# Experts get 96 row slots each: twelve steps of four 32-row blocks instead of sixteen steps of 128 rows, and a loop for rows past 96

## The chip, the cores and the metric

The kernel runs on one core of a Trainium2 chip. The metric is the device time of one execution in microseconds (us). The engines are named as in the profile: PE is TensorE (PEld its weight loads, that is the loads of its stationary operand), DVE VectorE, ACT ScalarE, POOL GpSimd, SP SyncE; a q behind a name is the engine's own queue of DMA issues and register work. All data is f32.

## The reference, cut to what matters

576 tokens (512 of a prompt, 64 of a sample) go through one layer: two recurrent branches and an output projection, then a mixture of experts, then a per-layer input embedding. The part around the change:

```python
grp = jnp.argmax(grp_logits, axis=-1)                      # top-1 group of 4
in_grp = ...                                               # the 4 experts of that group
top_v, top_i = lax.top_k(in_grp, TOP_K)                    # top 2 of them
w_top = jax.nn.softmax(top_v, axis=-1) * p_grp
...
for e in range(N_EXPERTS):                                 # 16 experts
    gu = jnp.einsum('bld,df->blf', u, w_gate_up[e])        # 1024 -> 512
    hid = jax.nn.silu(gu[..., :D_EXPERT]) * gu[..., D_EXPERT:]
    moe = moe + combine[..., e:e + 1] * jnp.einsum('blf,fd->bld', hid, w_down[e])   # 256 -> 1024
h = h + moe
u = rmsnorm(h, norm_ple)
h = h + jax.nn.sigmoid(u @ w_ple_gate) * (p_l @ w_ple_proj)
```

Each token uses two experts, so 1152 rows are spread over 16 experts. On the reference's inputs they fall as 65, 98, 80, 95, 44, 47, 51, 58, 61, 79, 68, 72, 88, 68, 87 and 91 rows.

## The kernel before, in words

Up to about 595 us the kernel does the branches, the output projection ("wo"), and the router. The router works tile by tile (five tiles of tokens, order 4, 1, 0, 3, 2): it ranks each token within its expert ("rank"), and turns ranks into a list of tokens for each expert with small matmuls ("ids"). The steps are written out by hand in `schedule()`; every engine walks that one list and does its part of each step. Two further kinds of step, "ovp" on DVE and "idv" on PE, prepare lists for rows past 128.

The expert stage works on 16 experts, one after the other, 128 row slots each. For expert e:

- POOL gathers its 128 token rows from `u_rows` in DRAM into `xg` (L2567; empty slots get row 0 with weight 0).
- PE transposes them into PSUM (`xpose`, L1222), DVE scales them into `xT` (L2284).
- PE does gate/up: 8 matmuls, k by k, with the 128 slots as stationary operand and 512 columns of `w_gu` moving, into PSUM bank `single[3]` (L1250). An f32 matmul leaves two records in the trace.
- ACT does SiLU (L1618), DVE the product (L2277, `hid`), PE two transposes (L1263), ACT copies them to `hT`.
- PE does down, 4 matmuls of 512 columns (L1234, `down`), but one expert later; ACT copies the result to `yb` and SP stores it to `y_slots` in DRAM.

Weights live in four buffers, one for an expert: gate/up 2 MB and down 1 MB. SP loads expert e+4 into the buffer of expert e right behind the store of e's result (`after_expert`, L667 to L670), which waits for that result. The first two experts are loaded during the router and before it, the third and fourth once the first two gathers have landed (L660).

After the last expert PE makes the p products of four tiles (L1290), reads from the table `ovi` how many blocks of rows past 128 there are, and goes through a loop over them (L1304 and following; SP, POOL, ACT and DVE have their halves of it; SP fetches the weights, POOL the rows). Then comes the tail: for each tile (order 0, 1, 4, 2, 3) POOL gathers the two rows of each token from `y_slots` (L2598), DVE adds them up (L2322, semaphore `h3`), PE transposes (L1336) and multiplies with `w_pg` (L1352), and ACT and DVE finish the tile. Gathers of the third and later tiles wait for the sum two tiles before.

## Time and profile before

| | |
|---|---|
| median of 3 runs | 873.87 us (873.84 to 874.2) |
| profiled execution, first to last instruction | 872.5 us |
| PE busy | 854.9 us, 98% |
| DVE / ACT / POOL busy | 388.7 / 223.3 / 155.1 us |
| DMA moved | 135.98 MB, mean 156 GB/s |
| granted PE clock, mean | 0.997 |

The profiled execution has no separate time of its own beside its span; the 1.4 us between the span and the median of the runs lie before the first and after the last instruction. Busy PE means that matmuls are under way; it is a share over stages with different limits, so the stages have to be read one by one.

### The profile page before, as it was taken

Reading aid. Unit: us, or ns where it says so; the run is one execution under the profiler, and the core shown is the slowest. Engines: PE = TensorE matmul, PEld = TensorE weight load, DVE = VectorE, ACT = ScalarE, POOL = GpSimd, SP = SyncE. Lnnn points to the kernel's source line nnn. Section 1 sums busy time; section 2 is a strip of 40 time slices with the busy share of each in tenths; the row PEclk is TensorE's granted clock in tenths of the full one; section 3 lists DMA queues with packets and bytes.
Section 4 is the critical chain, followed back from the end, with each engine's and each line's share of the span. In section 5 each row is a group of like instructions: output and inputs, shape, how many; then the busy total and the mean of one; then the engine's idle time right before and its main releaser. Section 6 shows DMA issues by size and latency. Waiting matters only on the chain.

```text
span 872.5 us, 11853 instructions
## 1 busy us (share of the span) xinstructions
PE 854.9 (98%) x4645; PEld 556.1 (64%) x4645; DVE 388.7 (45%) x857; ACT 223.3 (26%) x478; POOL 155.1 (18%) x186
## 2 busy tenths in 40 slices
PE   8999999999999999999999999999999999999996
PEld 4546777888799877777777764565444444444452
DVE  3223566677546324566734577364211111104553
ACT  2202152265224210121011101230311111125454
POOL 0324420022243314201300250002000000003000
PEclk9999999999999999999999999999999999999998
DMA  9521343502020201334132221157999999685211
GB/s 362 188 85 65 134 124 134 151 1 105 1 99 3 98 1 44 163 111 150 55 139 96 97 97 76 49 193 276 393 373 371 367 365 371 251 319 169 71 38 48
DMA packets 19814, 135.98 MB, mean 156 GB/s; under 512 B 2512, under 2 KB 3024, under 8 KB 12592
## 3 DMA queue, kind: packets, MB, share of 16 engines
q1 hardware_dynamic: 12176, 103.28, 30.9%
q0 software_dynamic: 5424, 26.45, 8.7%
q10 hardware_dynamic: 2160, 5.51, 2.1%
q8 instruction: 37, 0.61, 0.3%
q14 instruction: 17, 0.14, 0.1%
HBM read 117.83 MB, written 21.60 MB: 160 GB/s over the span
## 4 chain that ended last, share of the span: by engine, by line
PE 43%; DVE 3%; issue 2%; ACT 1%; DMA 1%; POOLq 0%; POOL 0%; DVEq 0%; ACTq 0%
PE single L1250 13%; PE pair L1234 6%; PE pair L1151 6%; PE single L914 6%; PE pair L1352 3%; PE pair L935 2%; PE single L1222 2%; PE pair L1290 2%; PE single L935 2%; PE single L1199 1%; DMA mem<-y_slots,posu 1%; PE single L1160 1%; DVE mem L2322 0%; PE single L1263 0%; DVE mem L2082 0%
## 5 line engine op out<-in xcount | busy, mean ns | idle before, releaser
L734 PE MATMUL pair<-mem 128*128 128x288 f32 x640 | 158.9, 408 | 0.0
L734 PEld LDWEIGHTS pair<-mem 128*128 128x128 f32 x640 | 120.3, 190 | 35.6 <-ACT mem L1373 2.1
L1250 PE MATMUL single<-mem 128*128 128x512 f32 x256 | 112.8, 593 | 0.8 <-DVE mem L2284 0.8
L914 PE MATMUL single<-mem 128*128 128x288 f32 x448 | 110.0, 407 | 0.3
L914 PEld LDWEIGHTS single<-mem 128*128 128x128 f32 x448 | 84.7, 190 | 25.7 <-issue 1.6
L1250 PEld LDWEIGHTS single<-mem 128*128 128x128 f32 x256 | 47.3, 190 | 54.1 <-issue 53.1
L1373 ACT ACTIVATE mem<-single 128x256 f32<-128x256 f32 (+5 forms) x113 | 46.5, 421 | 133.2 <-PE single L1160 48.7
L1373 ACT ACTIVATE mem<-pair 128x512 f32<-128x512 f32 (+5 forms) x85 | 37.8, 495 | 164.0 <-PE pair L734 63.1
L2277 DVE SCALAR_TENSOR_TENSOR mem<-single,mem 128x256 f32<-128x256 f32 x16 | 7.7, 483 | 138.8 <-PE single L1250 126.3
L1352 PE MATMUL pair<-mem 128*128 128x512 f32 (+1 forms) x192 | 63.4, 524 | 1.1 <-DVE mem L2332 1.1
L1234 PE MATMUL pair<-mem 128*128 128x512 f32 x128 | 57.7, 593 | 0.5 <-ACT mem L1373 0.5
L1151 PE MATMUL pair<-mem 128*128 128x512 f32 x112 | 51.0, 601 | 0.0
L1352 PEld LDWEIGHTS pair<-mem 128*128 128x128 f32 (+1 forms) x192 | 28.3, 172 | 33.3 <-issue 28.8
L2007 DVE TENSOR_TENSOR mem<-mem,single 128x288 f32<-128x288 f32 x40 | 18.1, 452 | 55.7 <-PE single L914 52.2
L2567 POOL DMA_INDIRECT mem<-u_rows,ids x16 | 15.8, 990 | 144.1 <-PE single L1222 134.0
L1234 PEld LDWEIGHTS pair<-mem 128*128 128x128 f32 x128 | 23.1, 190 | 24.1 <-issue 23.4
L1151 PEld LDWEIGHTS pair<-mem 128*128 128x128 f32 x112 | 20.3, 190 | 21.7 <-issue 21.4
L1618 ACT ACTIVATE mem<-single,mem 128x256 f32<-128x256 f32 x16 | 7.6, 475 | 103.6 <-PE single L1250 103.6
L809 PE MATMUL pair<-mem 128*128 128x512 f32 (+1 forms) x96 | 32.1, 525 | 0.0
L785 PE MATMUL pair<-mem 128*128 128x512 f32 x64 | 28.2, 595 | 0.9 <-DVE mem L1722 0.9
L935 PE MATMUL pair<-mem 128*128 128x288 f32 x112 | 28.4, 409 | 0.2
L1808 DVE SCALAR_TENSOR_TENSOR mem<-mem,vec 128x512 f32<-128x512 f32 x36 | 27.9, 774 | 1.3
(394 smaller groups left out, 1152.3 us busy)
## 6 DMA issues: line engine op xcount, KB each, us to landing
mem<-in_w_gu SPq DMA_DIRECT2D x16, 2048.0 KB, 9.1
mem<-in_w_down SPq DMA_DIRECT2D x16, 1024.0 KB, 11.8
y_slots<-mem SPq DMA_DIRECT2D x16, 512.0 KB, 3.7
y_slots<-in_zeros POOLq DMA_DIRECT2D x8, 512.0 KB, 8.4
mem<-in_w_ga SPq DMA_DIRECT2D x2, 2048.0 KB, 8.6
mem<-in_w_gb SPq DMA_DIRECT2D x2, 2048.0 KB, 8.4
mem<-in_w_wo SPq DMA_DIRECT2D x2, 2048.0 KB, 8.1
mem<-in_w_pg SPq DMA_DIRECT2D x2, 2048.0 KB, 11.5
```

Source lines behind the costliest of these rows:

```text
L734: last = nc.tensor.matmul(pb[:, hf, 0:HALF], w(k), rhs[:, k, hf * HALF:(hf + 1) * HALF], start=(k == 0), stop=(k == kk - 1))
L785: last = nc.tensor.matmul(q_bank[t][rows, cols], uT[:, k, t * P:t * P + ntok(t)], ring[0][:, 512 * k + cols.start:512 * k + cols.stop], st ...
L809: last = nc.tensor.matmul(pair[plan.buf[s]][rows, 0, cols], uT[:, k, t * P:t * P + ntok(t)], w[:, k, cols], start=(k == 0), stop=(k == KD ...
L914: last = nc.tensor.matmul(single[plan.buf[s]][:, 0:HALF], lhs[:, k, :], rhs[:, k, :], start=(k == 0 and j in (0, 1, 3, 4)), stop=(k == 3), ...
L935: last = nc.tensor.matmul(fast_bank(s), lhs[:, k, :], rhs[:, k, :], start=(k == 0 and j in (0, 1, 3, 4)), stop=(k == 1), skip_group_check= ...
L1151: last = nc.tensor.matmul(sx_bank[j], rows[:, u, v, :], wgt[:, u, 512 * v:512 * v + 512], start=(i == 0 and j < 5), stop=(i == 3), skip_gr ...
L1234: last = nc.tensor.matmul(pair[u % 2][:, n, :], hT[u % 2][:, k, :], w_dn[u][:, k, n * 512:(n + 1) * 512], start=(k == 0), stop=(k == 1))
L1250: last = nc.tensor.matmul(single[3][:, :], xT[u % 2][:, k, :], w_gu[u][:, k, :], start=(k == 0), stop=(k == KD - 1))
L1352: last = nc.tensor.matmul(pair[(k + 1) % 2][rows, hf, cols], u3T[:, c, t * P:t * P + n], w_pg[hf][:, c, cols], start=(c == 0), stop=(c == ...
L1373: copy = lambda out, in_, scale=1.0: nc.scalar.activation(out, in_, ACT.Copy, scale=scale)
L1808: V.scalar_tensor_tensor(out=acc[m % 2][:, 0:LP], in0=cbuf[m % 2][:, j:j + LP], scalar=conv_w[:, m, j:j + 1], in1=acc[m % 2][:, 0:LP], op0 ...
L2007: V.tensor_tensor(to, plus, single[plan.buf[s]][:, 0:HALF], ALU.add).then_inc(ev(k0), 1)
```

## The change

Each expert gets 96 slots (`CAP`) in blocks of 32 (`BS`). 16 x 96 = 1536 slots make 12 steps (`NPH`) of 128 slots. A step p has four blocks, each with its own expert: step 0 has three of expert 0 and one of expert 1, step 1 two of expert 1 and two of expert 2, step 2 one of expert 2 and three of expert 3, and so on in cycles of three steps and four experts. Gathers, transposes, DVE, ACT and stores work as before on 128 slots, twelve times. The matmuls of gate/up and down are cut into four, one for each 32 slots, each with the weights of its own expert moving and its own 32 rows of PSUM.

```diff
+def blocks_of(p):
+    return [((4 * p + g) // 3, (4 * p + g) % 3, g) for g in range(4)]
+def last_phase(e):
+    return (3 * e + 2) // 4
@@ PE, gate/up and down
-                    last = nc.tensor.matmul(single[3][:, :], xT[u % 2][:, k, :], w_gu[u][:, k, :],
-                                            start=(k == 0), stop=(k == KD - 1))
+                    for e, _, g in blocks_of(p):
+                        last = nc.tensor.matmul(single[3][BS * g:BS * g + BS, :], xT[p % 2][:, k, BS * g:BS * g + BS],
+                                                w_gu[e % 4][:, k, :], start=(k == 0), stop=(k == KD - 1))
...
-                        last = nc.tensor.matmul(pair[u % 2][:, n, :], hT[u % 2][:, k, :], w_dn[u][:, k, n * 512:(n + 1) * 512],
-                                                start=(k == 0), stop=(k == 1))
+                        for e, _, g in blocks_of(p):
+                            last = nc.tensor.matmul(pair[p % 2][BS * g:BS * g + BS, n, :], hT[p % 2][:, k, BS * g:BS * g + BS],
+                                                    w_dn[e % 4][:, k, n * 512:(n + 1) * 512], start=(k == 0), stop=(k == 1))
```

SP no longer waits for an expert's result before it reloads its gate/up weights, only for the step that used them last:

```diff
-            def after_expert(e, u, more):
-                sp.wait_ge(sem("y_ready"), 2 * e + 2)
-                sp.dma_start(y_slots[bass.ds(e * P, P), :], yb[u % 2]).then_inc(sem(f"y_stored{u % 2}"), 16)
-                if more:
-                    sp.dma_start(w_gu_flat[u], ...)
-                    sp.dma_start(w_dn_flat[u], ...)
+            for p in range(NPH - 1):
+                sp.wait_ge(sem("gu_mm"), p + 1)
+                for e in range(NEXP - 4):
+                    if last_phase(e) == p:
+                        load_gu(e + 4)
+                if p == NPH - 2:
+                    sp.dma_start(view(BLK, CHUNK_W), a["w_pg0"]).then_inc(sem("w_pg"), 16)
+                if p:
+                    store(p - 1)
+                for e in range(NEXP - 4):
+                    if last_phase(e) == p - 1:
+                        load_dn(e + 4)
+                if p == NPH - 3:
+                    sp.dma_start(w_proj.rearrange("p k c -> p (k c)"), a["w_proj"]).then_inc(sem("w_proj"), 16)
```

The preparation for rows past the slots moves out of the router: "ovp" and "idv" leave `schedule()`, and in their place DVE computes the lists behind step 0 and PE multiplies them out (ten matmuls of 64 columns) in step 1. The lists of slots for gathers are laid out by copies of 32 to 96 partitions:

```diff
-                    V.tensor_copy(ids[:, 0:NEXP], idp[0][:, 0:NEXP]).then_inc(sem("ids"), 1)
-                    V.tensor_copy(rsl[:, 0:NEXP], idp[0][:, NEXP:2 * NEXP]).then_inc(sem("ids"), 1)
+                    runs = {0: [(0, 0, 0, 96), (1, 0, 96, 32)], 1: [(1, 32, 0, 32), (1, 64, 32, 32), (2, 0, 64, 64)],
+                            2: [(2, 64, 0, 32), (3, 0, 32, 32), (3, 32, 64, 32), (3, 64, 96, 32)]}
+                    for v, dst in enumerate((ids, rsl)):
...
+                                last = V.tensor_copy(to[at:at + n, :, q], src[lo:lo + n, :, e])
+                            if v == 0:
+                                last.then_inc(sem("ids"), 1)
```

The loop for the rest takes blocks of 32 rows past 96 (up to 32 blocks, before 8 of 128 rows past 128) and now stands ahead of the p products. SP loads the block's expert anew; the weights move in four parts of the output columns, one to each column group, with the same 32 rows stationary:

```diff
+                    sp.dma_start(w_gu_flat[0], a["w_gu"][bass.ds(e * P, P), :]).then_inc(sem("ov_w"), 16)
+                    sp.dma_start(w_dn_flat[0], a["w_down"][bass.ds(e * P, P), :]).then_inc(sem("ov_w"), 16)
@@ PE, ahead of the p products
+                    pe.wait_ge(sem("ov_dve"), 2 * i + 1)
+                    pe.wait_ge(sem("ov_w"), 32 * i + 32)
+                    for k in range(KD):
+                        for g in range(4):
+                            last = nc.tensor.matmul(single[3][BS * g:BS * g + BS, 0:P], xT_ov[:, k, :], w_gu[0][:, k, P * g:P * g + P],
+                                                    start=(k == 0), stop=(k == KD - 1))
...
+                            last = nc.tensor.matmul(single[1][BS * g:BS * g + BS, 0:DE], hT_ov[:, BS * k:BS * k + BS],
+                                                    w_dn[0][:, k, DE * g:DE * g + DE], start=(k == 0), stop=(k == 1))
@@ ACT, the block's result
+                    for g in range(4):
+                        act.dma_start(y_slots[bass.ds(i * BS + NEXP * CAP, BS), DE * g:DE * g + DE], y_ov[BS * g:BS * g + BS, :])\
+                            .then_inc(sem("ov_stored"), 16)
@@ POOL, ahead of the tail's gathers
+                    pool.wait_ge(sem("ov_stored"), 64 * i + 64)
+                    pool.sem_inc(sem("ov_free"), 1)
```

How PE's program moves, at a place in the middle of the expert stage. Before, one expert (gate/up, transposes of the next expert's rows, down of the expert before, hidden transposes):

```order
L1250 MATMUL single<-mem 128x512 [waits hid,wgu1,xT]
L1250 MATMUL single<-mem 128x512 x7
L1222 MATMUL single<-const,mem 128x128 [waits xT,xg0]
L1222 MATMUL single<-const,mem 128x128 x7
L1234 MATMUL pair<-mem 128x512 [waits y_ready,hT]
L1234 MATMUL pair<-mem 128x512 x3
L1263 MATMUL single<-const,mem 128x128 [waits hid]
L1263 MATMUL single<-const,mem 128x128
```

Now one step, here one that uses the weight buffers 2 and 3:

```order
L1275 MATMUL single<-mem 32x512 [waits wgu3,hid,wgu2,xT]
L1275 MATMUL single<-mem 32x512 x31
L1245 MATMUL single<-const,mem 128x128 [waits xT,xg0]
L1245 MATMUL single<-const,mem 128x128 x7
L1260 MATMUL pair<-mem 32x512 [waits wdn2,y_ready,wdn1,hT]
L1260 MATMUL pair<-mem 32x512 x15
L1286 MATMUL single<-const,mem 128x128 [waits hid]
L1286 MATMUL single<-const,mem 128x128
```

The order is the same; gate/up and down have four times the instructions, and each step waits for the weights of two experts, gate/up and down apart.

SP's queue from the first reload on, now (three steps, then on in the same way):

```order
L680 DMA mem<-in_w_gu 128x4096 [waits gu_mm]
L680 DMA mem<-in_w_gu 128x4096
L702 DMA y_slots<-mem 128x1024 [waits y_ready]
L683 DMA mem<-in_w_down 128x2048
L680 DMA mem<-in_w_gu 128x4096 [waits gu_mm]
L702 DMA y_slots<-mem 128x1024 [waits y_ready]
L683 DMA mem<-in_w_down 128x2048 x2
L680 DMA mem<-in_w_gu 128x4096 [waits gu_mm]
L702 DMA y_slots<-mem 128x1024 [waits y_ready]
L683 DMA mem<-in_w_down 128x2048
```

Before, every expert had the same three rows there; two of them:

```order
L667 DMA y_slots<-mem 128x1024 [waits y_ready]
L669 DMA mem<-in_w_gu 128x4096
L670 DMA mem<-in_w_down 128x2048
L667 DMA y_slots<-mem 128x1024 [waits y_ready]
L669 DMA mem<-in_w_gu 128x4096
L670 DMA mem<-in_w_down 128x2048
```

Gate/up loads moved ahead of the store, down loads stay behind it, and four experts' loads now go with three stores.

PE's program behind the last down, before:

```order
L1290 MATMUL pair<-mem 128x512 [waits y_ready,w_proj,ld_p]
...
L1299 TENSOR_LOAD ovi [waits y_ready,ov_ready]
...
L1308 MATMUL single<-const,mem 128x128 [waits ov_xg]
...
L1313 MATMUL single<-mem 128x512 [waits ov_w]
...
L1336 MATMUL single<-const,mem 128x128 [waits h3]
```

and now:

```order
L1291 TENSOR_LOAD ovi [waits ov_ready]
...
L1297 MATMUL single<-const,mem 128x32 [waits ov_xg]
...
L1303 MATMUL single<-mem 32x128 [waits ov_w]
L1303 MATMUL single<-mem 32x128 x31
...
L1308 MATMUL single<-const,mem 128x64 [waits ov_dve]
...
L1312 MATMUL single<-mem 32x256 [waits ov_act]
L1312 MATMUL single<-mem 32x256 x7
...
L1330 MATMUL pair<-mem 128x512 [waits y_ready,w_proj,ld_p]
...
L1344 MATMUL single<-const,mem 128x128 [waits h3]
```

The loop (L1297 to L1312) moved from behind the p products (L1290, now L1330) to ahead of them.

## Rows read from the trace of the kernel before

**Rows 1.** Windows by stage: busy us of each engine, clock, DMA share, GB/s.

```profile
560.00:597.00 37.00, 35.73 (x186) 20.66 (x184) 21.77 (x88) 6.97 (x18) 4.32 (x5) 1.00 0.41 143
597.00:780.84 183.84, 183.37 (x549) 89.82 (x550) 33.07 (x82) 31.29 (x66) 13.89 (x16) 1.00 0.91 354
780.84:795.00 14.16, 13.74 (x33) 5.73 (x32) 2.57 (x2) 4.55 (x6) 4.04 (x5) 1.00 0.65 227
795.00:872.50 77.50, 69.25 (x248) 33.48 (x248) 38.15 (x60) 42.48 (x71) 6.29 (x6) 0.97 0.20 66
```

**Rows 2.** Chain that ended last, around two experts: start us, us, what.

```profile
606.59 6.87 PE single L1250 x16
...
652.18 6.87 PE single L1250 x16
659.05 0.87 PE single L1222 x8
659.92 3.44 PE pair L1234 x8
663.36 0.22 PE single L1263 x2
```

**Rows 3.** Windows, as in rows 1: weights alone, and ten steady experts.

```profile
608.00:612.00 4.00, 4.00 (x10) 1.71 (x9) 2.67 (x15) 0.00 (x0) 0.00 (x0) 1.00 1.03 418
641.70:755.70 114.00, 114.00 (x341) 55.59 (x340) 16.78 (x30) 18.41 (x41) 8.43 (x9) 1.00 0.95 367
```

**Rows 4.** Timeline of PE: start us, us to its last end, group.

```profile
96.70 2.19 PE L795 MATMUL pair<-mem 128*32 128x288 f32 x32
98.81 3.42 PE L734 MATMUL pair<-mem 128*128 128x288 f32 x13
...
580.20 0.65 PE L1169 MATMUL single<-mem,w_rt 128*32 128x128 f32 x16
```

**Rows 5.** Timelines of PE and DVE near the last router tiles.

```profile
581.36 0.71 PE L744 MATMUL pair<-mem 64*128 64x128 f32 x4
...
582.51 0.24 DVE L2153 SCALAR_TENSOR_TENSOR lg<-single,ms,vec 128x20 f32<-128x20 f32 x1 [0.74 <-PE single L1175]
```

**Rows 6.** Timeline of SP's DMA queue, the third expert's weights.

```profile
597.51 0.33 SPq L660 DMA_DIRECT2D mem<-in_w_gu  x1
```

**Rows 7.** DMA issues from 597 to 781 us: count, KB each, us to landing.

```profile
y_slots<-mem SPq DMA_DIRECT2D x15, 512.0 KB, 3.6
```

**Rows 8.** Timelines of DVE and PE, and ACT's groups by shape.

```profile
590.38 0.17 DVE L2204 TENSOR_SCALAR placeu<-placeu 128x6 uint32<-128x6 uint32 x1
590.87 0.96 DVE L2207 TENSOR_TENSOR mem<-mem,kr 128x768 f32<-128x768 f32 x1
...
308.69 1.08 PE L1089 MATMUL single<-mem 128*32 128x128 f32 x32
...
L1618 ACT ACTIVATE mem<-single,mem 128x256 f32<-128x256 f32 x16 | 7.6, 475 | 103.6 <-PE single L1250 103.6
L1373 ACT ACTIVATE mem<-single 128x128 f32<-128x128 f32 x2 | 0.5, 272 | 0.6 <-PE single L1169 0.6
```

**Rows 9.** Chain that ended last, end of the expert stage.

```profile
780.84 13.73 PE pair L1290 x32
...
795.00 1.11 PE single L1336 x8
```

**Rows 10.** Timeline of POOL, two gathers of the tail.

```profile
786.58 0.98 POOL L2598 DMA_INDIRECT mem<-y_slots,posu  x1 [22.47 <-SPq L701]
...
794.79 0.91 POOL L2598 DMA_INDIRECT mem<-y_slots,posu  x1 [3.46 <-DVE mem L2322]
```

**Rows 11.** The page's instruction queues (packets, MB, share), and a window of dense matmuls.

```profile
q8 instruction: 37, 0.61, 0.3%
q14 instruction: 17, 0.14, 0.1%
...
200.00:300.00 100.00, 98.39 (x1420) 88.33 (x1419) 56.71 (x141) 35.20 (x84) 34.41 (x51) 1.00 0.19 66
```

More of the change, by code:

```diff
@@ L736, in gemm_channels @@
                 last.then_inc(s_mm, 1)
-            def overflow_ids(t):
-                i, n = POS[t], ntok(t)
-                pe.wait_ge(sem("pickm"), 1 if i < 2 else 2)
-                for j in range(2):
-                    at = 128 * (2 * i + j)
-                    last = nc.tensor.matmul(idp[1], pickm[0:n, i, j, :], eov[0:n, at:at + 128],
-                                            start=(i + j == 0), stop=(i + j == NT))
-                return last
             pe.wait_ge(sem("rtmp_ones"), 1)
@@ L1208, in _, with overflow_ids @@
                     ev_wait(pe, s)
-            def late_overflow_ids():
-                for t in ORDER[2:]:
-                    last = overflow_ids(t)
-                last.then_inc(sem("idv_mm"), 1)
-            def xpose(n_gather, n_prev, u):
-                pe.wait_ge(sem(f"xg{u % 2}"), n_gather)
-                if n_prev is not None:
-                    pe.wait_ge(sem("xT"), n_prev)
+            def overflow_ids():
+                pe.wait_ge(sem("eov"), 1)
+                for c in range(2 * NT):
+                    n = ntok(ORDER[c // 2])
+                    last = nc.tensor.matmul(idp[1], pickm[0:n, c, :],
+                                            eov[0:n, c].rearrange("p v b -> p (v b)"), start=(c == 0), stop=(c == 2 * NT - 1))
+                last.then_inc(sem("ovi_mm"), 1)
@@ L1220, in xpose, with down @@
+            def xpose(p):
+                pe.wait_ge(sem(f"xg{p % 2}"), 16 * (p // 2 + 1))
+                if p:
+                    pe.wait_ge(sem("xT"), p)
                 for k in range(KD):
                     out = single[k // 4][:, (k % 4) * P:(k % 4 + 1) * P]
-                    last = nc.tensor.transpose(out, xg[u % 2][:, k * P:(k + 1) * P], C("ident"))
+                    last = nc.tensor.transpose(out, xg[p % 2][:, k * P:(k + 1) * P], C("ident"))
                 last.then_inc(sem("xT_mm"), 1)
-            def down(e, u, first):
-                pe.wait_ge(sem("hT"), e + 1)
-                if not first:
-                    pe.wait_ge(sem("y_ready"), 2 * e - 2)
-                elif u == 1:
-                    pe.wait_ge(sem("ids"), 4)
+            def down(p):
+                pe.wait_ge(sem("hT"), p + 1)
+                for e in experts_of(p):
+                    pe.wait_ge(sem(f"wdn{e % 4}"), 16 * (e // 4 + 1))
+                if p >= 2:
+                    pe.wait_ge(sem("y_ready"), 2 * p - 2)
+                if p == 1:
+                    pe.wait_ge(sem("ov_ready"), 3)
@@ new lines, in _ @@
+            xpose(0)
+            for p in range(NPH):
+                pe.wait_ge(sem("xT" if p else "xT_half"), p + 1)
+                for e in experts_of(p):
+                    pe.wait_ge(sem(f"wgu{e % 4}"), 16 * (e // 4 + 1))
+                if p:
+                    pe.wait_ge(sem("hid"), p)
+                for k in range(KD):
+                    if p == 0 and k == 4:
+                        xpose(1)
+                    for e, _, g in blocks_of(p):
+                        last = nc.tensor.matmul(single[3][BS * g:BS * g + BS, :], xT[p % 2][:, k, BS * g:BS * g + BS],
+                                                w_gu[e % 4][:, k, :], start=(k == 0), stop=(k == KD - 1))
+                last.then_inc(sem("gu_mm"), 1)
+                if 0 < p < NPH - 1:
+                    xpose(p + 1)
+                if p == 1:
+                    overflow_ids()
+                if p:
+                    down(p - 1)
+                pe.wait_ge(sem("hid"), p + 1)
@@ L1262, in expert @@
                 for k in range(2):
-                    last = nc.tensor.transpose(single[2][:, k * P:(k + 1) * P], hid[u % 2][:, k * P:(k + 1) * P], C("ident"))
+                    last = nc.tensor.transpose(single[2][:, k * P:(k + 1) * P], hid[p % 2][:, k * P:(k + 1) * P], C("ident"))
                 last.then_inc(sem("hT_mm"), 1)
-            xpose(16, None, 0)
-            for e in range(4):
-                expert(e, e, True, True, (16 * ((e + 1) // 2 + 1), 32))
-            with pe.Fori(1, 3) as i:
-                for u in range(4):
-                    expert(4 * i + u, u, True, False, ((i * 2 + (u + 1) // 2 + 1) * 16, i * 32 + 32))
```

415 lines of the change are left out of this document (190 added, 225 removed).

## The prediction

> **What bounds the kernel now.** I read the windows by stage first [rows 1]. In the expert stage, 597.0 to 780.8 us, TensorE is busy 183.37 of 183.84 us at the full granted clock (1.00, the 2.4 GHz level); the DMA engines are busy 0.91 of it. Then come 14.2 us of p products (a matmul stage of four tiles) and 77.5 us of tail with DMA nearly idle. The chain that ended last [rows 2] runs through TensorE alone there and shows one expert: 6.87 us of gate/up, 0.87 of transposes, 3.44 of down, 0.22 of hidden transposes, 11.40 us in all, sixteen times. So TensorE sets the stage. But DMA is close behind: in ten steady experts its share is 0.95 at 367 GB/s, and where it has a backlog of weights it is 1.03 (full) at 418 GB/s [rows 3]. A change that shortens TensorE's part by a quarter therefore meets the DMA engines, and the sum has to be made for both.
>
> **Does the new shape run at the old speed?** A step has 4 x 8 gate/up matmuls with 32 stationary columns and 512 moving ones where an expert had 8 with 128. If the four column groups run at once, gate/up still takes 6.87 us; one after another, 27.5. The trace of before has 32-column matmuls: L795, 32 records of 288 moving columns with four different moving operands, begins at 96.70 and the next group begins at 98.81 [rows 4]. (A matmul in f32 leaves two records.) L734 behind it, 128 columns wide with the same 288 moving, starts a record every (3.42 - 0.41) / 12 = 0.25 us, 0.41 being the mean of one. 32 x 0.25 = 8.0 us in turn, 2.0 at four at a time; it took 2.11. So the groups overlap, and 0.1 to 0.2 us goes at the change of shape. L1169 says the same: 16 records of 128 columns are over in 0.65 us; in turn they would take 16 x 128 / 288 x 0.25 = 1.8. A step changes shape four times; I charge 0.1 each, 0.4. Step = 11.40 + 0.4 = 11.8 us.
>
> The Trainium skill has a measured figure that speaks against this ("TensorE: Matmul & The Clock Gate", Part 3, Packing small matmuls): four 32-row tiles with 512 moving columns gave 3.07x, not 4x, and column tiling behaves within some ns of that. By it a step would be about 10.3 / 0.77 + 1.5 = 14.9 us. L795's 8.0 / 2.11 = 3.8x, its shape change included, disagrees, so the sum keeps 11.8.
>
> **TensorE's side.** Before the stage the change drops two matmul groups (idv) and two pieces of DVE work (ovp), and cuts the id copy into small ones. Only the idv of tile 4 shows on the path: DVE stood 0.74 us for the transposes (L1175) queued right behind it [rows 5]. The copy for gather 0 is now two copies; call it +0.1. I take 0.5 us off: step 0's gate/up starts at 596.5. Step 0 has gate/up and a transpose but no down: G0 (its end of gate/up) = 604.9, and step 1 starts at 606.4 after SiLU, hidden product and transposes, as before (606.59) [rows 2]. Step 1 carries the ten small matmuls that place rows past 96, +1.0. The DVE work for them is about 18 small operations at 0.17 to 0.2 us and 2,560 elements of wide ones at the rate of L2207 (768 in 0.96) [rows 8]: 6.5 us, from 606.1 to 612.6, before TensorE asks at 614.5: hidden behind step 1's gate/up, margin 2 us; without that cover it would delay down(0) one for one. If weights were always there, gate/up of step p would end at G1 = 613.4, then every 11.8 (step 1 being a us longer): G5 = 661.7, G11 = 732.5, last down at about 741.
>
> **The DMA side.** Sixteen experts' weights are still 3.146 MB each; only gathers and stores fall from 16 to 12. The third expert's load is issued at 597.51 after the first gathers have landed [rows 6], unchanged by the diff. From there to the end of the weights that the row loop at the end needs, the engines must move: 14 experts 44.0 MB, w_proj 1.05, w_pg0 2.1, pT 0.6, one expert again for the loop 3.15: 50.9 MB at 418 GB/s = 121.8 us. A store plus a gather costs what the steady experts leave [rows 3]: 11.4 x 0.95 - 3.146 / 0.418 = 3.3 us a pair; ten pairs = 33 us. Sum 154.8: 597.5 + 154.8 = 752.3, plus 1.5 to 2 us to land (a lone store lands in 3.6 us though it is 1.8 of work) [rows 7]: **754.5**. This holds only if the queue is never empty. I followed it: loads of expert e+4 go out when e's last gate/up is over, its down weights some 6 us later behind the store. At each issue 6 us or more of older work is still queued (gu5 goes out at 613.4, the queue is full to 621; gu6 and gu7 at 626.4, full to 634; later 10 us), so it isn't.
>
> Put together, TensorE waits twice: step 6 for expert 9, which lands at 670 instead of the wanted 666.5, and step 9 for expert 13, at 710.5 instead of 705. That gives G9 = 717.5, G10 = 729.3, G11 = 741, last down over at **749**, where before has 780.84 [rows 9]. The stage alone is 32 us shorter; TensorE without waits would be 40.
>
> **The loop at the end.** Routing the reference's own inputs gives 98 rows for expert 1 and at most 95 for any other: one block of 32 is past 96, none was past 128, and before's loop shows no instruction. The body runs once. SP issues its weights near 735.5, behind dn15, w_proj, w_pg0 and store 9, hence 754.5. TensorE does its 8 transposes before and then waits 5 to 6 us. Then: 64 records of 128 columns at four at a time 1.8 to 2.1 us (L1089, half as many, 1.08 to its last end), SiLU and copy 0.45, product 0.25, transpose 0.3, copy 0.25, 16 records of 256 columns 0.95, five hops 0.3, register work 0.2: 4.5 us, so it ends at 759. Before ran the p products (13.73 us) straight after the last down; now they run 759 to 772.8. Beside them: copy 0.4, four DMA issues on ACT 1.4 (at SP's 0.33), landing about 3 on busy engines, POOL's pT4 0.75, so tile 0's first gather starts near 765 instead of 786.58. From it to the next gather that waits for tile 0's sum is 8.2 us in before (794.79 [rows 10]): 773.5. That is 0.7 us later than the products, and the tail (L1336) starts at **774** instead of 795.0. w_pg1 and the norm land near 765. The tail is untouched: 77.5 us. Span 872.5 - 21 = 851.5; the runs' median stands 1.4 us over the profiled span, so 852.9; I round up to **853.5** for hops not counted.
>
> **Rivals.** (1) Column groups overlap worse, as the skill's figure says. By rows: gate/up and down take 1.3 times their 10.3 us, a step is 14.9; DMA no longer limits; last down 613.4 + 1 + 10 x 14.9 + 9 = 772, tail starts 18.9 later at 791, time 870. For it: no row has four groups of 512 columns under a full DMA load. Against: L795. 0.08, and 0.12 for halfway, 13 us a step: last down 753 by the same sum, but the block's weights come at 754.5 anyway, time 855 to 862. (2) Slower: TensorE starves for instructions. The stage has some 2,700 instructions for it, all unrolled. At 16 KB a packet and some 64 bytes an instruction (0.75 MB on the two instruction queues [rows 11] for the page's 11,853) that is 11 fetches, behind full DMA engines; with smaller packets up to 20. If each of 15 stopped it for a store's landing, 3.6 us, that is 54 us: last down 741 + 54 = 795, tail at 814, time 893. It decides from 2.3 us a fetch, 35 us in all. Against: between 200 and 300 us TensorE took 1420 matmul records, 14 a us, and was busy 98.39, where this stage asks 9 a us; but DMA was 0.19 then. 0.06; all slower cases 0.08. (3) The DMA reckoning is off: a share of 0.95 instead of full adds 8 us: 861; 0.12, in the range. (4) The loop doesn't run, because the counts differ: the products start at 749, the gathers 5.7 us later as in before, tail near 763.5: 843; 0.05. A second block would instead cost a serial 17 us (weights 7.5, landing 2, body 4.5, store 3), 870; 0.02. (5) Forecast, 849 to 857: 0.55.
>
> **How the numbers follow.** The likeliest case gives 853.5. The low end takes in part of the case without a block and a full rate a little above 418, 845; the high end takes in the DMA at 0.95 and the halfway case with some tail cost, 864. The rest lies above. Within 0.2% (1.7 us, about what a measurement tells) only rival 1 with extras: 0.03. Faster 0.89, slower 0.08.
>
> **What would show it.** After: 32x512 groups with 64 records in 6.9 to 7.1 us; waits for weights at steps 6 and 9 of 3 to 5 us and none before; DMA share over 0.97 from 600 to 755; the loop's gate/up released by a DMA near 755; p products about 14 us after 759; tail start near 774 and 77.5 long. It is wrong if a step is longer than 13 us without a weight wait, if gaps on TensorE are put down to issue, if DMA falls idle in the stage, or if the last gathers come later than the products.

## The result and the profile after

| | before | after |
|---|---|---|
| time, median of 4 runs, us | 874.04 (873.84 to 875.23) | 848.81 (846.25 to 851.14) |
| profiled execution: time, span, us | (above) | 849.0, 847.2 |
| ratio after / before | | 0.9705 [0.9682, 0.9728] |
| mean granted clock | | 0.994 |

The kernel became 2.95% faster, 4.7 us more than forecast. The windows of the changed kernel, from the first expert step to the tail (span, then busy us of PE, PEld, DVE, ACT and POOL, granted clock, DMA share, GB/s), answer to [rows 1, 3]:

```profile
597.00:641.70 44.70, 43.43 (x382) 16.24 (x386) 17.38 (x56) 7.90 (x15) 3.73 (x5) 1.00 1.00 405
641.70:744.30 102.60, 101.86 (x906) 33.34 (x898) 13.56 (x24) 16.09 (x35) 7.37 (x10) 1.00 1.01 418
744.30:749.00 4.70, 0.69 (x12) 0.57 (x8) 0.42 (x1) 1.08 (x2) 0.00 (x0) 0.95 1.04 437
749.00:752.50 3.50, 3.35 (x64) 2.88 (x64) 0.00 (x0) 0.00 (x0) 0.00 (x0) 0.57 0.99 420
...
755.30:758.00 2.70, 2.70 (x8) 1.15 (x5) 0.00 (x0) 0.39 (x1) 0.00 (x0) 0.52 0.27 94
...
761.00:771.00 10.00, 10.00 (x26) 4.45 (x25) 2.57 (x2) 2.77 (x3) 5.04 (x6) 1.00 0.62 216
```

Read them down. From 641.7 to 744.3 two resources are full at once: TensorE is busy 101.86 of 102.60 us, the DMA share is 1.01. Then TensorE stands still for 4.1 us, and the clock is at 0.57 and 0.52, near its lower level (0.50, 1.2 GHz), in the windows in which it next has much work; after 761 it is back at 1.00. The chain that ended last shows one step, and what replaced the old end of the stage [rows 2, 9]:

```profile
644.99 0.37 PE single L1286 x2
645.35 7.00 PE single L1275 x64
652.36 1.02 PE single L1245 x8
653.38 3.57 PE pair L1260 x32
...
733.15 15.89 DMA mem<-in_w_down
749.08 3.40 PE single L1303 x64
...
755.34 15.63 PE pair L1330 x32
770.96 0.87 PE single L1344 x8
```

A step takes 7.00 + 1.02 + 3.57 + 0.37 = 11.96 us, 11.97 from one start to the next, against 11.40 for an expert before. The block's weights, landing at 749.05, release the loop; the p products run to 770.96, and behind them come 847.2 - 770.96 = 76.2 us of tail, where before had 77.5. The chain stays on TensorE there until 839.9 us; the last 7.3 us are ACT's and DVE's work on the last tile. The table of waits says how little TensorE waited between 600 and 772 us (us in total, times, longest):

```profile
PE single L1303 <- DMA mem<-in_w_down: 4.1, 1, 4.1
...
PE single L1275 <- DMA mem<-in_w_gu: 0.3, 1, 0.3
```

One wait for an expert's weights in twelve steps, of 0.3 us (step 9, at 705.46). What full engines do to the transfers stands in the DMA summary of 590 to 760 us (count, KB each, us from issue to landing):

```profile
y_slots<-mem SPq DMA_DIRECT2D x12, 512.0 KB, 11.1
...
mem<-u_rows,ids POOLq DMA_INDIRECT x12, 11.0
y_slots<-mem ACTq DMA_DIRECT2D x4, 32.0 KB, 1.5
```

A store of 512 KB that landed in 3.6 us before [rows 7] now takes 11.1, and a gather 11.0. The engines move 405 to 418 GB/s meanwhile, so this isn't slower work but a longer line. Nothing on TensorE waits for them in the stage, because each is asked for a whole step ahead.

### The profile page after: what moved, and what is told of

Its sections match the earlier page's. It is cut to its first block and busy times, and to the rows that moved or that the text cites. A ratio compares the mean times of both kernels' runs of the same rounds, so it can differ in the third digit from the quotient of the medians.

```text
span 847.2 us, 13448 instructions
## 1 busy us (share of the span) xinstructions
PE 822.9 (97%) x5462; PEld 519.9 (61%) x5462; DVE 385.5 (46%) x857; ACT 215.2 (25%) x464; POOL 152.6 (18%) x184
## 5 line engine op out<-in xcount | busy, mean ns | idle before, releaser
L765 PEld LDWEIGHTS pair<-mem 128*128 128x128 f32 x640 | 120.3, 190 | 35.6 <-ACT mem L1381 2.1
L935 PE MATMUL single<-mem 128*128 128x288 f32 x448 | 110.0, 407 | 0.3
L935 PEld LDWEIGHTS single<-mem 128*128 128x128 f32 x448 | 84.7, 190 | 25.7 <-issue 1.6
L1275 PE MATMUL single<-mem 128*32 128x512 f32 x768 | 85.1, 594 | 1.1 <-DVE mem L2304 0.9
L1381 ACT ACTIVATE mem<-pair 128x512 f32<-128x512 f32 (+5 forms) x77 | 33.5, 485 | 156.7 <-PE pair L765 63.0
L1275 PEld LDWEIGHTS single<-mem 128*32 128x32 f32 x768 | 24.0, 110 | 52.7 <-issue 51.6
L2297 DVE SCALAR_TENSOR_TENSOR mem<-single,mem 128x256 f32<-128x256 f32 x12 | 5.8, 484 | 104.3 <-PE single L1275 91.4
L1172 PE MATMUL pair<-mem 128*128 128x512 f32 x112 | 51.0, 601 | 0.0
L1260 PE MATMUL pair<-mem 128*32 128x512 f32 x384 | 43.7, 595 | 0.5 <-ACT mem L1381 0.5
L1172 PEld LDWEIGHTS pair<-mem 128*128 128x128 f32 x112 | 20.3, 190 | 21.7 <-issue 21.4
L2586 POOL DMA_INDIRECT mem<-u_rows,ids x12 | 11.4, 947 | 110.5 <-PE single L1245 100.5
L806 PE MATMUL pair<-mem 128*128 128x512 f32 x64 | 28.2, 595 | 0.8 <-DVE mem L1735 0.8
L956 PE MATMUL single<-mem 128*128 128x288 f32 x112 | 27.8, 406 | 0.0
## 6 DMA issues: line engine op xcount, KB each, us to landing
mem<-in_w_down SPq DMA_DIRECT2D x17, 1024.0 KB, 14.9
y_slots<-mem SPq DMA_DIRECT2D x12, 512.0 KB, 11.1
```

Source lines behind the costliest of these rows:

```text
L765: last = nc.tensor.matmul(pb[:, hf, 0:HALF], w(k), rhs[:, k, hf * HALF:(hf + 1) * HALF], start=(k == 0), stop=(k == kk - 1))
L806: last = nc.tensor.matmul(q_bank[t][rows, cols], uT[:, k, t * P:t * P + ntok(t)], ring[0][:, 512 * k + cols.start:512 * k + cols.stop], st ...
L935: last = nc.tensor.matmul(single[plan.buf[s]][:, 0:HALF], lhs[:, k, :], rhs[:, k, :], start=(k == 0 and j in (0, 1, 3, 4)), stop=(k == 3), ...
L956: last = nc.tensor.matmul(fast_bank(s), lhs[:, k, :], rhs[:, k, :], start=(k == 0 and j in (0, 1, 3, 4)), stop=(k == 1), skip_group_check= ...
L1172: last = nc.tensor.matmul(sx_bank[j], rows[:, u, v, :], wgt[:, u, 512 * v:512 * v + 512], start=(i == 0 and j < 5), stop=(i == 3), skip_gr ...
L1260: last = nc.tensor.matmul(pair[p % 2][BS * g:BS * g + BS, n, :], hT[p % 2][:, k, BS * g:BS * g + BS], w_dn[e % 4][:, k, n * 512:(n + 1) * ...
```

## The experiments

My theory after the result: (T1) the gain is TensorE's alone, twelve steps of 12.0 us instead of sixteen of 11.4; (T2) DMA doesn't set the stage though its share is 1.01, it sets only what stands behind it, the block's weights; (T3) the 4.1 us wait and the slow clock behind it are the loop's real price. Rivals: the column groups lose time by themselves; the gain comes from the new order of SP's loads; DMA sets the stage. Ratios are to the kernel before, with runs on the same chip; intervals are 95%.

**a_cols: before, with column groups and nothing else.** Sixteen experts of 128 slots, each matmul of gate/up and down cut into four groups of 32.

```diff
-                    last = nc.tensor.matmul(single[3][:, :], xT[u % 2][:, k, :], w_gu[u][:, k, :],
-                                            start=(k == 0), stop=(k == KD - 1))
+                    for g in range(0, P, 32):
+                        last = nc.tensor.matmul(single[3][g:g + 32, :], xT[u % 2][:, k, g:g + 32], w_gu[u][:, k, :],
+                                                start=(k == 0), stop=(k == KD - 1))
... (down in the same way)
```

> The kernel before, sixteen experts of 128 slots, with one part of the change alone: gate/up and down are cut into four matmuls of 32 stationary columns each (same weights four times). Theory 1 (column groups overlap fully, a change of shape costs 0.14 us as in the changed kernel's trace): an expert takes 11.40 + 0.56 = 11.96 us, the stage grows by 16 x 0.56 = 9 us, time near 883. Rival (the overlap is poorer when the moving operand is read by four groups under full DMA, and the changed kernel hides it in fewer steps): by the skill's 3.07 of 4, 3.1 us an expert, time near 923. Second rival (instructions run short): gaps on TensorE put down to issue, some us each.

Measured: 885.14 us (882.46 to 885.9), 1.0106 [1.0084, 1.0129]. Its chain, and a window of ten experts:

```profile
752.75 7.00 PE single L1252 x64
759.75 1.02 PE single L1222 x8
760.78 3.57 PE pair L1235 x32
764.35 0.37 PE single L1265 x2
```

```profile
641.70:761.00 119.30, 119.30 (x1060) 39.58 (x1056) 16.84 (x31) 18.35 (x40) 9.05 (x10) 1.00 0.91 351
```

The reader is to see the same four durations as in the changed kernel, and gate/up and down with four times as many matmul records as in [rows 2], at 11.96 us an expert instead of 11.40. Each of the four groups is 0.13 to 0.15 us longer than in before, and that is all; TensorE is never idle in the window, so no instruction comes late. I had put 883. The cutting by itself costs 1.1%; it pays only because a quarter of the steps goes.

**g_before_order: before, with the new order of loads and nothing else.** SP asks for gate/up weights when the last gate/up that used the buffer is over, ahead of the store.

```diff
-            for e in range(4):
-                after_expert(e, e, True)
...
+            for e in range(13):
+                if e < 12:
+                    sp.wait_ge(sem("gu_mm"), e + 1)
+                    sp.dma_start(w_gu_flat[e % 4], a["w_gu"][(e + 4) * P:(e + 5) * P, :]).then_inc(sem(f"wgu{e % 4}"), 16)
+                if e:
+                    after_expert(e - 1, (e - 1) % 4, False)
+                    sp.dma_start(w_dn_flat[(e - 1) % 4], a["w_down"][(e + 3) * P:(e + 4) * P, :]).then_inc(sem(f"wgu{(e - 1) % 4}"), 16)
```

> The kernel before with the other part of the change alone: gate/up weights of expert e+4 are issued when e's gate/up is over, down weights behind the store of the next step, all loads and stores of SP unrolled. Theory 1 (TensorE sets the stage before, loads come in time anyway): same time, 874, DMA share 0.95 as before. Rival (the gain of the changed kernel comes in part from a fuller DMA queue): some us faster.

Measured: 875.25 us (873.82 to 877.15), 1.0008 [0.9996, 1.0019]. No effect: TensorE had its weights in time without it.

**e_half: the changed kernel with half of each gate/up load left out** for experts 4 to 15 (the columns not loaded hold the weights of an earlier expert, so these experts compute with partly wrong weights). 12.6 MB less, TensorE's work unchanged.

```diff
-                sp.dma_start(w_gu_flat[e % 4], a["w_gu"][e * P:(e + 1) * P, :]).then_inc(sem(f"wgu{e % 4}"), 16)
+                c = CHUNK_W if e < 4 else CHUNK_W // 2
+                sp.dma_start(w_gu_flat[e % 4][:, 0:c], a["w_gu"][e * P:(e + 1) * P, 0:c]).then_inc(sem(f"wgu{e % 4}"), 16)
```

> The changed kernel with half of each gate/up load left out for experts 4 to 15 (the other half of the buffer keeps the weights of four experts earlier), so that 12.6 MB less move; the loop's own load is whole. TensorE's program is the same. Theory 1 (TensorE sets the stage at 12 us a step, DMA only the loop's wait): the last down ends at 744 as before, the loop's weights are there, clock stays full; time 842, the same as moving w_pg. Rival (the full DMA engines set the stage): 12.6 MB at 415 GB/s are 30 us, the stage ends near 715 to 720, time near 820.

Measured: 844.88 us (844.63 to 846.28), 0.9659 [0.9636, 0.9681]. One window of its stage, its last down (L1261) and the loop's gate/up, and the last down of the changed kernel (L1260):

```profile
600.00:740.00 140.00, 138.80 (x1231) 47.24 (x1223) 30.32 (x77) 22.58 (x47) 10.19 (x13) 1.00 0.87 332
...
740.90 3.64 PE L1261 MATMUL pair<-mem 128*32 128x512 f32 x32 [0.47 <-ACT mem L1382]
...
747.25 2.00 PE single L1304 x64
...
740.74 3.64 PE L1260 MATMUL pair<-mem 128*32 128x512 f32 x32 [0.47 <-ACT mem L1381]
```

With DMA at 0.87 instead of full, the last down ends where it did: 147.0 us behind the start of step 0 (597.58), in the changed kernel 147.3 (597.07), and the 0.3 us are its one wait. DMA doesn't set the stage (T2 holds; otherwise 12.6 MB less, some 30 us at 417 GB/s, would have shown). The 4 us come from behind it, 3 less than I had put (842): the block's weights land 1.8 us earlier, the wait is 2.1 us, and the loop's gate/up takes 2.00 us instead of 3.40, at full clock.

**b_noloop: the changed kernel with the number of blocks set to 0**; it leaves out the two rows of expert 1 past 96. **c_order: w_pg0 loaded behind the block's weights**, not ahead of them. **d_warm: five matmuls of 512 columns that nobody reads, in the wait.**

```diff
 b: count of blocks
-float(BS - 1 - CAP), 0.0, ALU.add, ALU.max
+-4096.0, 0.0, ALU.add, ALU.max
 c: SP
-                if p == NPH - 2:
-                    sp.dma_start(view(BLK, CHUNK_W), a["w_pg0"]).then_inc(sem("w_pg"), 16)
...
                     sp.dma_start(w_dn_flat[0], a["w_down"][bass.ds(e * P, P), :]).then_inc(sem("ov_w"), 16)
+            sp.dma_start(view(BLK, CHUNK_W), a["w_pg0"]).then_inc(sem("w_pg"), 16)
             store(NPH - 2)
 d: PE, in the loop
+                    for _ in range(5):
+                        nc.tensor.matmul(single[2][:, :], C("ones"), h2[:, 0, 0:512], start=True, stop=True)
                     pe.wait_ge(sem("ov_dve"), 2 * i + 1)
                     pe.wait_ge(sem("ov_w"), 32 * i + 32)
```

> The changed kernel with the count of blocks past 96 forced to zero, so that the loop is skipped; it leaves out the two rows of expert 1 past its 96 slots. It prices the whole loop. Theory 1 (the loop costs its wait for weights 4.1, its body 6.3, and 1.9 of slower p products, but without it the tail's first gathers become late): last down at 744.3, products over at 758, first sum at 760, span 836, time 838, 11 us less. Rival (DMA sets the end of everything, and the loop's weights only stand in a queue that is full anyhow): the tail waits for w_pg and the stores, time no lower than 843.

> The changed kernel with one load moved: the first w_pg chunk is issued behind the loop's weights instead of ahead of them. Theory 1 (the loop waits 4.1 us because 5.0 us of w_pg stands ahead of its weights in the queue, and the idle time then lowers the clock): weights land at 744, no wait, clock 1.00 throughout, body 4.5 us, products 13.7 us, time near 842. Rival A (the clock falls for another reason, such as the loop's small matmuls): the wait is gone but the body and the products keep 3.4 and 15.6 us, time 844.5. Rival B (w_pg becomes late for the tail): time as the changed kernel's, 849.

> The changed kernel with five matmuls of 512 columns, results unused, put in the wait for the loop's weights (4.3 us of work in a wait of 4.1). It changes nothing but what TensorE does in the wait. Theory 1 (the idle wait lowers the granted clock, 0.57 in two stretches behind it, and that costs 1.6 us in the loop's gate/up and 1.9 in the p products): those come back, gate/up 1.9 us, products 13.7 us, time 3 us less, near 846. Rival (the body is slow through its instructions and hops, and the clock plays no part): no change, 849.

Measured: b 846.17 us (843.44 to 847.49), 0.9673 [0.9656, 0.9689]; c 848.36 us (847.99 to 850.77), 0.97 [0.9681, 0.972]; d 848.09 us (847.4 to 848.57), 0.9687 [0.9671, 0.9703]. All three intervals touch that of the changed kernel, 0.9705 [0.9682, 0.9728]: b may be a little faster, c and d can't be told from it. I had put b at 838, c at 842 and d at 846 (its rival at 849): b and c are misses, and for d the times don't tell the two cases apart. The traces say more, if one thing is kept in mind. The profiled executions reach the expert stage at different times, though the edits of c and d lie behind that point and b's changes one constant: step 0's first matmul starts between 597.07 and 600.44 us (the latest is j_noloop's, below). So times of two traces are compared here as they stand behind that start:

| | step 0 starts | tail starts | from one to the other | step 0 to the end of the span |
|---|---|---|---|---|
| before | 596.98 | 795.00 | 198.0 | 275.5 |
| changed kernel | 597.07 | 770.96 | 173.9 | 250.1 |
| b_noloop | 598.56 | 763.65 | 165.1 | 243.0 |
| c_order | 598.23 | 768.53 | 170.3 | 248.4 |
| d_warm | 599.14 | 770.24 | 171.1 | 247.6 |
| e_half | 597.58 | 766.23 | 168.7 | 245.3 |

These are single executions; two of the changed kernel (here and after_again below) differ by 0.4 to 0.5 us. First d, two windows of it:

```profile
749.00:752.00 3.00, 3.00 (x38) 1.52 (x40) 0.00 (x0) 0.00 (x0) 0.00 (x0) 1.00 1.04 440
...
755.00:758.00 3.00, 3.00 (x21) 1.38 (x22) 0.00 (x0) 0.38 (x1) 0.00 (x0) 1.00 0.51 200
```

The same program on a TensorE that was kept busy: clock 1.00 where it was 0.57 and 0.52. Its chain, with its start of step 0 first and TensorE's p products from its timeline last:

```profile
599.14 3.64 PE single L1275 x32
...
746.71 4.49 PE single L1300 x10
751.20 1.93 PE single L1305 x64
...
758.09 2.03 DMA y_slots<-mem
...
763.31 5.50 DMA mem<-y_slots,posu
...
770.24 1.09 PE single L1346 x8
...
755.91 14.00 PE L1332 MATMUL pair<-mem 128*128 128x512 f32 x32
```

The loop's gate/up is 1.93 us, not 3.40, and the products take 14.00, not 15.7: the idle wait was what lowered the clock, both times. Counted from step 0 the products end at 170.8 instead of 173.9, 3.1 us earlier, and the tail starts 2.8 us earlier: the clock's price is as T3 had it, though the run times show no more than a hint of it. The last 0.3 us are missing because it is no longer the p products that release the tail: it is the loop's result, stored, gathered and summed. Behind the loop stand **two chains**, PE's products and store, gather, sum. In the changed kernel the second ended with this sum:

```profile
767.87 1.28 DVE L2338 SCALAR_TENSOR_TENSOR mem<-mem,wcomb 128x1024 f32<-128x1024 f32 x1 [1.35 <-DMA mem<-y_slots,posu]
```

It is over at 769.15, 1.8 us before the products. Shortening the products alone gives only that distance; whatever the loop's body gains, both chains gain. c_order's chain says it louder:

```profile
746.39 1.99 PE single L1302 x64
...
753.35 5.39 DMA y_slots<-mem
...
767.19 1.30 DVE mem L2337
...
768.53 1.24 PE single L1343 x8
769.77 3.36 PE pair L1329 x16
...
770.00:771.00 1.00, 1.00 (x6) 0.47 (x4) 1.00 (x2) 0.00 (x0) 0.86 (x1) 0.50 0.58 131
```

Here the wait for weights is gone (gate/up starts at 746.39, 3.9 us earlier counted from step 0) and the clock is 1.00 in the loop. But w_pg0 and w_pg1 are still moving when the block's result, four pieces of 32 KB, wants to be stored: a piece lands 5.0 us after its issue (median, the last one 5.39), 1.5 in the changed kernel. The tail waits 3.4 us for the sum, and behind this wait the clock is at 0.50 again (from 770 to 772 us; the last line is the window of its first us): the 16 matmuls of L1329 take 3.36 us, 1.88 in the changed kernel. So the tail starts 3.6 us earlier and the end is only 1.8 us earlier. T3 is wrong in its size: wait and clock together, 7 us, are not to be had by moving this load. In b, without a loop, the last step's store takes the same place, queued behind w_pg1:

```profile
746.70 8.27 DMA y_slots<-mem
...
757.09 5.13 DMA mem<-y_slots,posu
...
763.65 1.97 PE single L1344 x8
```

The Trainium skill ("DMA: Bandwidth & Descriptors", Issuing engines are not separate DMA queues) says that transfers of SP, ACT and POOL run on the same 16 engines and interleave, whoever issued them. These rows agree: ACT's own queue did not keep 32 KB pieces clear of SP's 2 MB loads, 5.0 us beside them against 1.5 without.

**f_two: a second block, which finds no rows.** It tells what a block costs where nothing hides it.

```diff
-float(BS - 1 - CAP), 0.0, ALU.add, ALU.max
+float(BS + 1 - CAP), 0.0, ALU.add, ALU.max
```

> The changed kernel with the block count rounded up two rows earlier, so that expert 3 with 95 rows gets a block too (an empty one) and the loop runs twice. It prices one more block. Theory 1 (a further block is serial: store landed, weights issued, 7.5 us of load and 2 to land, body 6 us, then its own store): 17 to 20 us more, time 866 to 869. Rival (the second block overlaps with the p products or the stores): under 10 us more.

Measured: 872.8 us (871.29 to 874.48), 0.9972 [0.9959, 0.9985]: 24 us more than with one block, where I had put 17 to 20. Its chain from the first block's result on:

```profile
760.62 1.47 DMA y_slots<-mem
...
763.53 10.66 DMA mem<-in_w_down
774.23 3.57 PE single L1303 x64
...
780.66 15.63 PE pair L1330 x32
```

From one block's gate/up (751.02) to the next (774.23) are 23.2 us: body 8.0 to 759.0, issue and store 3.1, SP's turn 1.4, weights 10.7. SP asks for the second block's weights only when the first one's result is stored, so nothing overlaps, and the clock is low again (3.57, 15.63). Almost the whole gain of the change is gone with the second block.

**h_best: c_order with pT4 issued behind the first gathers on POOL. i_pool: c_order, and w_pg1 and pT4 issued by POOL behind the second tile's gathers**, so that they are in nobody's way before the tail; PE waits for w_pg1 where it first needs it. **j_noloop: b_noloop with the last store ahead of w_pg1** (leaves out the same two rows). **after_again: the changed kernel once more**, on the chip of i and j.

```diff
 i: SP
-            sp.wait_ge(sem("gu_mm"), NPH)
-            sp.dma_start(view(BLK + 12288, CHUNK_W), a["w_pg1"]).then_inc(sem("w_pg"), 16)
             store(NPH - 1)
 i: POOL, in the tail's gathers
+                if k == 1:
+                    pool.wait_ge(sem("dn_mm"), NPH)
+                    pool.wait_ge(sem("ld_p"), 16)
+                    pool.dma_start(pT4, a["pT"][:, :, 4 * P:TOK]).then_inc(sem("ld_p"), 16)
+                    pool.dma_start(view(BLK + 12288, CHUNK_W), a["w_pg1"]).then_inc(sem("ld_iota"), 16)
 j: SP
+            store(NPH - 1)
             sp.dma_start(view(BLK + 12288, CHUNK_W), a["w_pg1"]).then_inc(sem("w_pg"), 16)
-            store(NPH - 1)
```

> The changed kernel with w_pg behind the loop's weights and, besides, POOL's small load pT4 moved behind the first two gathers of the tail. Theory 1: 842 from the order, and 0.5 to 0.8 us less if the first sum of the tail is what its start waits for then: 841 to 842. Rival (the gathers have slack): as the order alone.

> The changed kernel with the loop's weights ahead of the first w_pg chunk, and with the second w_pg chunk and pT4 taken from their places ahead of the tail's gathers and issued by POOL behind the gathers of the second tile. Theory (the tail starts at the later of two chains: TensorE's p products, and the loop's result stored, gathered and summed; moving w_pg alone won nothing since its loads then lay on that store, 5.4 us to land instead of 2.0, and on the last step's store): the store lands in 2 to 3 us, first gathers at 757 instead of 761, products over and first sum both near 765, against 771.0 in the changed kernel; time 843. Rival (the gathers are held by something else, and the second chain stays at 769): time 847.

> The kernel without the loop (it leaves out the two rows past 96) with the last step's store issued ahead of the second w_pg chunk instead of behind it. Theory of the two chains: without the loop the tail waited for the last store, which took 8.3 us behind w_pg; now it lands in some 3 us, first gathers at 751, first sum near 758.5, products over at 759.5: tail starts at 759.5 instead of 763.6, time 842. Rival: as the kernel without the loop, 846.

> The changed kernel itself on the same chip, for the comparison with the two others: 848 to 849.

| | median us | ratio to before | span us | tail starts | behind the start of step 0 | step 0 to the end |
|---|---|---|---|---|---|---|
| h_best | 846.61 (845.98 to 847.42) | 0.9676 [0.9654, 0.9698] | 844.2 | 767.75 | 169.3 | 245.8 |
| i_pool | 846.15 (845.58 to 848.41) | 0.9675 [0.9661, 0.9689] | 844.9 | 765.28 | 167.0 | 246.6 |
| j_noloop | 842.12 (841.42 to 844.13) | 0.9623 [0.961, 0.9636] | 842.3 | 764.29 | 163.9 | 241.9 |
| after_again | 850.28 (848.89 to 851.65) | 0.9722 [0.9709, 0.9736] | 847.1 | 770.79 | 173.4 | 249.7 |

i_pool and h_best are the fastest versions that compute everything: i_pool is 0.5% below the changed kernel on the same chip (0.9675 / 0.9722 = 0.995, intervals apart). The two can't be told apart. Both missed what I had hoped from the chains (841 to 842, and 843); j_noloop came as forecast (842). In i_pool the forecast up to the tail came true:

```profile
751.35 13.93 PE pair L1327 x32
765.28 0.89 PE single L1341 x8
```

But its tail is 844.9 - 765.28 = 79.6 us, 3.4 longer than the changed kernel's 76.2, and its table of waits from 765 to 845 us shows where:

```profile
PE pair L1359 <- DVE mem L2347: 2.0, 2, 1.1
PE pair L1327 <- DMA mem<-in_pT: 1.1, 1, 1.1
```

The first row is TensorE waiting for DVE. DVE's sums waited 6.2 us for gathers in that stretch (2.7 in the changed kernel's tail), and a gather took 6.7 us to land (5.3), while w_pg1 took 12.2 on the same engines. That w_pg1 is what makes them late is likely, but no run takes it apart. In j the store is quick, and the gather behind it pays instead:

```profile
748.59 3.05 DMA y_slots<-mem
...
753.75 9.11 DMA mem<-y_slots,posu
```

Store 8.27 and gather 5.13 in b, store 3.05 and gather 9.11 in j: 13.4 and 12.2 us. Where the 2 MB are queued decides who waits for them, and hardly how long. j's own gain over b is 0.5%, with intervals that don't overlap (0.9623 against 0.9673), on another chip; the two traces, counted from step 0, are 1.1 us apart.

## Why the prediction was right, and where it was off

It gave 853.5 in 845 to 864; 848.8 came. The main mechanism held: the column groups run at once, so twelve steps replace sixteen, and one serial block with its products stands behind them. What failed is that DMA would hold TensorE up by 8.5 us in the stage; it held it up by 0.3. That the number came so close is in part luck: against those 8.2 us stand 4.0 of TensorE's own work in the stage and 3.7 behind it that the sum had too low. Point by point:

- **Do column groups run at once?** Yes. Gate/up of a step is 7.00 us, not 27.5, as L795 and L1169 had said [rows 4]. The change of shape was charged 0.1 and costs 0.13 to 0.15: a step is 11.97, not 11.8 us, over eleven steps 1.9 us more. a_cols shows it apart from all else. Rival 1 is refuted: by the Trainium skill's 3.07 ("TensorE: Matmul & The Clock Gate", Part 3, Packing small matmuls) a step would be 14.9 us, and outside step 1 with its extra matmuls no run here shows more than 12.0.
- **Before the stage.** Step 0 starts at 597.07 instead of 596.5. The lists for rows past 96 are on DVE from 606.36 to 612.67, as forecast to 0.1 us, and hidden. The small matmuls that place them were put at 1.0 us and take 2.5 (L1234, 20 records at 0.125 us): I had priced them by their 64 moving columns, but a record with 128 of them takes no more, 0.87 / 8 = 0.11 us in the transposes of [rows 2], which leave one record each.
- **The DMA side, the step that failed.** I had TensorE wait 3.5 us at step 6 and 5 us at step 9. It waited 0 and 0.3. The term that was mis-sized is the pair of a store and a gather, 3.3 us, taken from ten experts with a share of 0.95 at 367 GB/s [rows 3]. With the queue full, all traffic moved at the rate that I had kept for weights alone: 418 GB/s from 641.7 to 744.3 us. At that rate the pair's 1.05 MB is 2.5 us, ten pairs 25 instead of 33, and the weights would come 8 us earlier than forecast. The 405 GB/s up to 641.7 us take 1.4 of that back; the other 1.1 us stay open. The loop's weights came at 749.05 instead of 754.5, and those of experts 9 and 13 cost a wait of 0 and 0.3 us. So the last down ended at 744.3: the 741 of TensorE's side, plus 0.6 for the start, 1.5 for the placing and 1.9 for the shapes, less rounding. That TensorE sets the stage, but for 0.3 us, is shown by e_half, which takes a fifth of the stage's traffic away (332 instead of 417 GB/s) and leaves the last down in its place.
- **The loop.** Its body was put at 4.5 us and the products at 13.7; they took 6.3 (749.08 to 755.34) and 15.63. Of the missing 3.7 us 3.1 are the clock, at 0.57 after 4.1 us of idle TensorE; the other 0.6 are mis-sized terms, since body and products take 4.7 and 14.0 us at full clock too (d_warm). I had forecast a wait of 5 to 6 us there and put its price for what follows at nothing. d_warm shows the cause: with dummy work in the wait the loop's gate/up takes the 1.9 us forecast.
- **The start of the tail.** Forecast 774, measured 771.0: 5.5 earlier for the weights, 3.7 later for body and products, 0.7 less because the gathers don't come last, and the rest rounding. The prediction had both chains in it, 772.8 and 773.5; that they were so close was its warning, and I overlooked it when I put c_order at 842, nearly 7 us below the changed kernel.
- **The tail** was said to be untouched, 77.5 us, and was 76.2. Before had waits of TensorE for DVE there, 1.5 us together, that are not in the trace of after. That the earlier gathers gave DVE a lead is the likely reason; no run tests it.
- **Rival 2**, instructions that come late, didn't show: TensorE had 1060 records in 119.30 us of a_cols and no gap. **Rival 4**, no block, was put at 843; b gave 846.2 and j 842.1. The second block was put at 17 us and takes 23.2 from one to the next: its weights 10.7 and not 9.5, the body 8.0 at the low clock and not 4.5, and SP's turn 1.4 that I had left out.
- **Where the rest of the gain is.** The stage is 36.5 us shorter (780.84 to 744.3). Between its end and the tail lie 26.7 us now (744.3 to 770.96), 14.2 before. These 12.5 us stand where the loop runs ahead of the products: 4.8 of transposes and waiting, 6.3 of body, 1.9 of slower products, less 0.4 that before had between products and tail. i_pool gets 4 us back and j, without any loop, 8 (846.2 and 842.1 against 850.3 on one chip). That is less than the 12.5, because the chain of store, gather and sum then stands in the loop's place: in j the tail starts at 764.29, 16.9 us behind the last down, and TensorE waits 3.0 us for the sum.

What stays open: whether the changed kernel needs the new order of SP's loads (g tests it in the kernel before only, where TensorE leaves DMA more room); and how the 16 DMA engines share a 2 MB load with gathers of many small rows. b, c, i and j only show that the sum hardly changes. And a version that prefetches the second block's weights, which f_two calls for, was not tried.

## What to carry to other kernels

Cutting a matmul of 128 stationary columns into four column groups of 32 is nearly free where the four stand next to each other (0.56 us in 11.4 here, over the four groups of a step), so slots can be given out by 32 where the rows allow it; but count on what the remainder costs, since one serial block with its own weights is 24 us, and two of them eat the gain of a quarter of the steps. Where two chains meet at an instruction, work out both ends before hoping for the gain of one, and price a DMA that is moved as work that goes to whoever now stands beside it. A wait on TensorE can cost more than itself (4.1 us here, and 3.1 more for the clock behind it), so fill it with work; to put work there that is needed anyway, such as the p products, was not tried. And compare two traces from a point that both share, ahead of the edit: here they reached the stage up to 3.4 us apart.

## What was not expected of the hardware

- The granted clock fell twice in the changed kernel, each time to 0.50, the level of 1.2 GHz: from 749 to 752, at the end of 4.1 us without matmuls, and again from 756 to 758, though TensorE had been busy 3.35 of 3.50 us (749.0 to 752.5) and 1.28 of 2.80 (752.5 to 755.3) between and had 1.00 in the second of these. Windows of 1 us:

```profile
750.00:751.00 1.00, 1.00 (x25) 0.92 (x21) 0.00 (x0) 0.00 (x0) 0.00 (x0) 0.50 0.99 426
...
754.30:755.30 1.00, 1.00 (x17) 0.42 (x17) 0.00 (x0) 0.00 (x0) 0.00 (x0) 1.00 0.37 152
...
757.00:758.00 1.00, 1.00 (x3) 0.45 (x2) 0.00 (x0) 0.00 (x0) 0.00 (x0) 0.50 0.19 52
```

In e_half the wait was 2.1 us and the clock stayed: 2.00 us for the same 64 records. In d_warm neither fall came, with the same gaps in the body, so the second one hangs on the wait too; how, no run shows. The Trainium skill ("TensorE: Matmul & The Clock Gate", Part 1) has it that the throttled state is the default and activity releases it; the fall after the wait and d_warm agree with that.
- DMA with a long line before it (a store landed 11.1 us after its issue) moved weights, stores and gathers together at 418 GB/s for 103 us, as fast as weights alone [rows 3]. The same mix had made 367 GB/s at a share of 0.95.
- Stores of 32 KB landed in 1.5 us in the changed kernel and in 5.0 beside 2 MB loads issued on another engine's queue (c_order); a gather took 5.1 us in b and 9.1 in j, where the 2 MB load is queued behind the last store instead of ahead of it.
- Ten f32 matmuls with 64 moving columns took 2.5 us (L1234), 0.125 a record, where a transpose, one record with 128 moving columns, takes 0.11; next to these, fewer columns bought nothing.
